# Other tiles take the dense path, one batch's first v rows are summed by TensorE in column groups, and the dense weights are built during the queries

## The reference, cut to what matters

```
z = rmsnorm(x) @ w_in          # pool channels | q | k | v | gate_pool | gate_attn
x += (sigmoid(gate_pool) * (pool(z) @ w_pool_out) + sigmoid(gate_attn) * (attention(q,k,v) @ w_attn_out)) @ w_out
h = rmsnorm(x)                 # the expert layer, per token:
q = h @ w_query                # 8 heads, two halves of 128
s = q . sub_keys               # 16 halves x 128 scores; top 16 of each half, then top 16 of the sums
idx, gate = top16, softmax     # 8 heads x 16 = 128 experts of 16384
x += sum_k gelu(h . expert_u[idx_k]) * gate_k * expert_v[idx_k]
y = rmsnorm(x)
```

## Time and profile before

| | us |
|---|---|
| median of three runs | 3104.01 (3103.43 to 3106.72) |
| the profiled execution | 3107.14 |
| its span, first to last instruction | 3105.3 |

### The profile page before, as it was taken

One profiled execution on the slowest core, in us unless ns is written; L12 is line 12 of the kernel. 1 busy time (PEld: TensorE's weight loads), 2 busy tenths in 40 slices (PEclk: granted clock), 3 DMA queues, 4 the chain that ended last, 5 costly groups with the idle time before them and its releaser, 6 DMA issues.

```text
span 3105.3 us, 34626 instructions
## 1 busy us (share of the span) xinstructions
PE 2701.4 (87%) x9441; PEld 1579.9 (51%) x9441; DVE 2230.3 (72%) x4681; ACT 572.9 (18%) x983; POOL 1633.7 (53%) x1444
## 2 busy tenths in 40 slices
PE   7989989793455867949799899999999999999997
PEld 6885566472133445524366555555555545545553
DVE  1446678999988777998888677777777766655554
ACT  2322401210034101112266211111111111100001
POOL 0001553366677776557522566666666656645441
PEclk9999999896666888969899999999999999999999
DMA  4385796788789998877677999999999999998894
GB/s 149 115 250 176 253 372 231 256 298 295 247 309 321 328 380 331 273 229 273 216 267 268 342 401 402 403 399 402 389 395 390 368 382 403 401 333 322 327 322 164
DMA packets 360702, 961.16 MB, mean 310 GB/s; under 512 B 28064, under 2 KB 152736, under 8 KB 359072
## 3 DMA queue, kind: packets, MB, share of 16 engines
q0 software_dynamic: 184320, 671.17, 58.9%
q1 hardware_dynamic: 175136, 284.69, 26.4%
q10 hardware_dynamic: 1152, 4.19, 0.3%
HBM read 930.58 MB, written 29.36 MB: 309 GB/s over the span
## 4 chain that ended last, share of the span: by engine, by line
PE 62%; DVE 21%; issue 5%; DMA 5%; ACT 4%; POOL 3%; POOLq 0%; ACTq 0%; SPq 0%; DVEq 0%
PE o_bank L778 21%; PE bank L788 21%; PE bank L550 9%; DVE ring L1116 8%; PE bank L538 5%; DMA ring<-in_expert_u,idx_now 3%; POOL ring L1083 2%; PE bank L724 2%; PE o_bank L759 2%; DVE region_q L1347 2%; DVE region_q L1352 2%; DVE region_q L1356 2%; DMA wslot<-in_expert_uT 1%; ACT region_q L983 1%; PE bank L528 1%
## 5 line engine op out<-in xcount | busy, mean ns | idle before, releaser
L1083 POOL DMA_INDIRECT ring<-in_expert_u,idx_now x640 | 783.9, 1225 | 432.8 <-DVE dots L1116 196.1
L1083 POOL DMA_INDIRECT ring<-in_expert_v,idx_now x640 | 744.3, 1163 | 472.7 <-issue 152.3
L778 PE MATMUL o_bank<-region_b,wslot 128*128 128x384 f32 x2048 | 686.5, 489 | 17.0 <-DMA wslot<-in_expert_uT 17.0
L788 PE MATMUL bank<-wslot,region_q 128*128 128x512 f32 x1536 | 679.9, 592 | 0.0
L1116 DVE CUSTOM_DVE_ANT_0 ring<-ring,h 128x1024 f32<-128x1024 f32 x512 | 608.1, 1221 | 73.6 <-DMA ring<-in_expert_u,idx_now 61.0
L1429 DVE SCALAR_TENSOR_TENSOR region_c<-ring,dots,region_c 128x1024 f32<-128x1024 f32 x384 | 493.0, 1284 | 100.4 <-DMA ring<-in_expert_v,idx_now 60.3
L778 PEld LDWEIGHTS o_bank<-region_b,wslot 128*128 128x128 f32 x2048 | 391.4, 191 | 318.9 <-issue 63.6
L788 PEld LDWEIGHTS bank<-wslot,region_q 128*128 128x128 f32 x1536 | 291.8, 190 | 340.3 <-issue 306.6
L1075 POOL COPY idx_now<-idx 128x8 uint32 x160 | 105.4, 659 | 519.6 <-DVE idx L1358 286.3
L724 PE MATMUL bank<-ring,region_s 128*128 128x512 f32 x512 | 246.0, 610 | 57.2 <-ACT region_s L961 47.0
L1003 ACT ACTIVATE region_q<-o_bank 128x384 f32<-128x384 f32 x128 | 62.9, 491 | 982.8 <-PE o_bank L778 939.7
(11 more groups left out here) (163 smaller groups left out, 2363.5 us busy)
## 6 DMA issues: line engine op xcount, KB each, us to landing
wslot<-in_expert_uT SPq DMA_DIRECT2D x128, 512.0 KB
wslot<-in_expert_v SPq DMA_DIRECT2D x128, 512.0 KB
wslot<-in_w_in SPq DMA_DIRECT2D x34, 1024.0 KB
wslot<-in_w_query SPq DMA_DIRECT2D x24, 1024.0 KB
region_p<-expert_weights SPq DMA_DIRECT2D x20, 768.0 KB
wslot<-in_w_out SPq DMA_DIRECT2D x12, 1024.0 KB
expert_weights<-region_q SPq DMA_DIRECT2D x6, 2048.0 KB, 7.4
expert_weights<-region_p SPq DMA_DIRECT2D x6, 2048.0 KB, 7.4
```

What stands on the lines that cost most here:

```text
L778: ins = nc.tensor.matmul(dense_in[q][:, 0:DENSE_T], u_cols[slot][:, k, :], h2T[:, k, T - DENSE_T:T], start=(k == 0), stop=(k == KD - 1))
L788: ins = nc.tensor.matmul(dense_out[2 * t + n][:], hidden[q][:, t * P:(t + 1) * P], v_cols[slot][:, n * 512:(n + 1) * 512], start=start, st ...
L1083: nc.gpsimd.indirect_dma_start(ring[:, r, :], None, table, bass.IndirectOffsetOnAxis(ap=idx_now[:, half, r:r + 1], axis=0)).then_inc(row_l ...
```

## The change

The tiles are divided anew. Gathered are now tiles 0 and 1 of batch 0 and tiles 0 to 2 of batch 1, dense are tiles 2 and 3 of batch 0 and tile 3 of batch 1: five and three, as before.

- The u and v rows of the two gathered tiles of batch 0 are all handled ahead of the columns. The order on POOL is u0, v0, u1, v1 and then u2, u3, u4, v2, v3, v4 beside the columns: 512 rows ahead of them and 768 beside them (`ROWS_BY`: 6.14 for each of 125 columns, none for the first three).
- The v rows of the two early tiles are gathered by token: one indirect DMA brings the 128 expert rows of one token, one to a partition. The ids are turned (transposed) for that. The weights of a token then are the stationary operand of a matmul, as one column among 32, the rest zeros; four tokens, for four groups of 32 columns of the array, make a "quad" of 8 matmuls of 512 columns (`sum_rows`). 32 quads make a tile, 64 in all. They stand between batch 1's projections (24), at the end of group 1's queries (8), in batch 1's queries (18) and beside the last weights (14).
- The dense weights of the two batch-0 tiles are built between batch 1's queries (64 jobs of four tokens), those of the third after them (32 jobs). ACT issues the stores. Blocks are of 16 tokens, units of 8 columns.
- Batch 1's tile 3 is merged first; the other three merges are made beside the columns, at columns 0, 6 and 26, with one column (and its rows) at each of eight pauses (three columns in the first merge).
- POOL takes its ids straight from `idx`, with no copy to `idx_now`, and its loop is written out. Waits on one count of used rows become one semaphore for each place of the ring.

The diff, cut to its core:

```diff
-GATHERED = (TT, 1)
-BLOCK = 32
-UNIT_COLS = 4
-UNITS_BESIDE = {(0, 1): 3, (1, 0): 3, (1, 1): 4}
-SUMMED = 1
+GATHERED = ((0, 0), (0, 1), (1, 0), (1, 1), (1, 2))
+DENSE = ((0, 2), (0, 3), (1, 3))
+EARLY = 2
+GATHERS = [("u", 0), ("v", 0), ("u", 1), ("v", 1), ("u", 2), ("u", 3), ("u", 4), ("v", 2), ("v", 3), ("v", 4)]
+BLOCK = 16
+UNIT_COLS = 8
+QUARTERS = 4
+SUM_BUFS = 4
+FIRST_ROWS = 3
+ROWS_BY = [max(0, (j - FIRST_ROWS + 1) * LATE_ROWS // (N_KEYS - FIRST_ROWS)) for j in range(N_KEYS)]
+MERGE_AT = {6: 3, 26: 4}
...
+            def sum_rows(*key):
...
+                for r in quads:
+                    rows = [ROW["v", k] + QUARTERS * r + q for q in range(QUARTERS)]
+                    for n in rows:
+                        landed(pe, n)
+                    pe.wait_ge(sum_w_ready, k * QUADS + r + 1)
+                    for half in range(2):
+                        for q, n in enumerate(rows):
+                            ins = nc.tensor.matmul(sums[half][q * QUAD_ROWS:(q + 1) * QUAD_ROWS, :],
+                                                   sum_w[:, r % SUM_BUFS, q, QUAD_ROWS - 1 - r:2 * QUAD_ROWS - 1 - r],
+                                                   ring[:, n % RING, half * 512:(half + 1) * 512],
+                                                   start=(r == 0), stop=(r == QUADS - 1), skip_group_check=True)
...
                 for c in range(HALVES // 2):
                     for hp in (2 * c, 2 * c + 1):
                         feature_major((g, "query", hp), (g, "query", c), h2T, hp % 2 * P, KD)
+                        builds(c, hp % 2)
...
+                        builds(c, 2 + hp % 2)
+                    if WT_AFTER.get(g) == c:
+                        turn_weights(g, g - 1)
+                    sum_rows("query", g, c)
...
-                                nc.gpsimd.tensor_copy(
-                                    idx_now[:, half, :],
...
+            def column():
...
+                j = columns[0]
+                weigh_column()
+                rows(ROWS_BY[j] - (ROWS_BY[j - 1] if j else 0))
...
-            attn_out(1, 3)
+            pool_out(1, 1)
             attention(1, 1)
+            attn_out(1, 6)
             out(1, 3)
...
-            merge(0, 3, 6)
-            rotate(1, 3)
-            pool_out(2, 3)
-            attention(2, 3)
-            attn_out(2, 7)
-            out(2, 5)
+            merge(0, 3)
+            rotate(1)
+            pool_out(2, 2)
+            add_sums(0)
+            split_ids(0)
+            attention(2, 1)
+            attn_out(2, 6)
+            out(2, 4)
             norm2(2)
...
+            merge(1, 3)
+            softmax(1, slice(3, 4))
+            split_ids(2)
+            for n in range(2 * JOBS_PER_TILE, W_JOBS):
+                one_hots(n)
+            add_sums(1)
+            norm2_again(4)
+            pauses = iter(range(8))
+            merge(1, 0, lambda: column() if next(pauses) in (3, 5, 7) else None)
+            while columns[0] < N_KEYS:
+                if columns[0] in MERGE_AT:
+                    merge(*GATHERED[MERGE_AT[columns[0]]], column)
+                else:
+                    column()
```

More of the change, by code:

```diff
@@ new lines @@
+LATE_SUMS_AT = {**{("query", 2, c): 3 for c in range(2, 8)}, ("h2D",): 4, ("chosen",): 2, **{("w", n): 1 for n in range(67, 96, 4)}}
+SUMS_BEFORE, SUMS_OF = {}, {}
+for _k, _table in enumerate((SUMS_AT, LATE_SUMS_AT)):
+    _n = 0
+    for _key, _count in _table.items():
+        SUMS_BEFORE[_key], SUMS_OF[_key] = (_k, _n), (_k, range(_n, _n + _count))
+        _n += _count
+    assert _n == QUADS and max(_table.values()) <= SUM_BUFS
+FIRST_ROWS = 3
+LATE_ROWS = (len(GATHERED) - EARLY) * 2 * SLOTS
@@ L554, in turn_h, with build_weights @@
+            def build_weights(n):
+                g = LAST_GROUP[1]
+                pe.wait_ge(one_hot_ready, n + 1)
+                bank = fill(g, "w", n)
+                for r in range(TOKENS_EACH):
+                    at1 = n % 2 * TOKENS_EACH + r
+                    ins = nc.tensor.matmul(bank[:, r * P:(r + 1) * P], one_hot_i[:, at1, :], one_hot_j[:, at1, :],
+                                           start=True, stop=True)
+                done(ins, g, "w", n)
             def turn_h(g):
@@ L769, in take_column @@
+            sum_rows("h2D")
+            turn_chosen(2)
+            sum_rows("chosen")
+            for n in range(2 * JOBS_PER_TILE, W_JOBS):
+                build_weights(n)
+                sum_rows("w", n)
             def take_column(j, slot, turn):
@@ new lines, in dot, with add @@
+                dotted[0] += count
+            added = [EARLY * SLOTS]
+            def add(count):
+                for d in range(added[0], added[0] + count):
+                    k, s = divmod(d, SLOTS)
+                    b, t = GATHERED[k]
+                    n = ROW["v", k] + s
+                    landed(dve, n)
+                    if s:
+                        used(dve, n - 1)
+                    x = x1s[b][:, t, :]
+                    nc.vector.scalar_tensor_tensor(out=x, in0=ring[:, n % RING, :],
+                                                   scalar=dots[:, DOTS_AT[k] + s:DOTS_AT[k] + s + 1], in1=x,
+                                                   op0=ALU.mult, op1=ALU.add).then_inc(slot_used[n % RING], 1)
+                added[0] += count
@@ L1132, in norm1, with rows @@
+            def rows(count):
+                dots_left = min(count, len(GATHERED) * SLOTS - dotted[0])
+                dot(dots_left)
+                add(count - dots_left)
             def norm1(b):
@@ new lines, in weigh, with add_sums @@
+            def weigh(k):
+                b, t = GATHERED[k]
+                dve.wait_ge(gelu_ready, k + 1)
+                d = dots[:, DOTS_AT[k]:DOTS_AT[k] + SLOTS]
+                nc.vector.tensor_tensor(d, d, gate[:, b, t, :], ALU.mult).then_inc(weighed, 1)
+                dve.wait_ge(weighed, k + 1)
+            def add_sums(k):
+                b, t = GATHERED[k]
+                all_used(dve, ("v", k))
+                for half in range(2):
+                    x = x1s[b][:, t, half * 512:(half + 1) * 512]
+                    n = step(nc.vector.tensor_tensor(x, x, sums[half], ALU.add))
+                after(n)
+                dve.sem_inc(sums_added, 1)
@@ L1528, in _ @@
-            dot(4)
-            norm2(2)
-            dot(8)
-            for hp in range(HALVES):
-                top_halves(2, hp)
-                dot(4)
-            dot_to(GATHERED[0] * SLOTS // BODY)
-            softmax(0)
-            weigh(0)
-            for t in range(TT):
-                merge(1, t)
-            softmax(1)
-            for t in range(GATHERED[1], TT):
-                split_ids(t)
-            for block in range(BLOCKS):
-                one_hots(block)
-            add_sums()
```

824 lines of the change are left out of this document (442 added, 382 removed).

## The result

The changed kernel takes 3016.72 us (median of four runs, 3012.2 to 3028.44), the kernel before 3105.36 beside it: a ratio of 0.9721, interval 0.9692 to 0.9749. It is faster by 89 us, where 200 were forecast. The range ended at 3010. Its profiled execution takes 3016.6 us with a span of 3014.8.

What follows compares the result with a forecast made beforehand. PE bounded the columns before, waits the front; after, DMA at 400 to 412 GB/s would pace the columns. Fourth column's add at 1492, plus 1388, 5 and a tail of 20 gave 2905 us; range 2805 to 3010.

Steps and rivals of the forecast that it cites:

- attention of batch 1 starts: Front, after group 1, batch 1's projections, rotate and pool_out: attention was to start at 854 us instead of 868.9.
- the queries: Batch 1's queries with weight jobs and quads: 230 us instead of 125.1, from 1101 to 1331.
- from there to the fourth column's add: Last halves, merge, third tile's 32 weight jobs and first columns: from 1331 to column 3's add at about 1492.
- the columns from there: 125 columns, paced by DMA: 1388 us, 109 at 10.95 and 16 at 12.1, plus 5 for the last add.
- the price that decides most: PE time of one quad of 8 matmuls: 1.7 us if its four column groups run together; 64 quads cost 110 us.
- the ends of 3.4 and 6.9: Quad price in us if column groups run only in pairs (3.4, chance 0.06) or one after another (6.9, chance 0.05).
- 6 x 30: Six query chunks of batch 1 with three quads each, taken at 30 us; with 2 x 24.8 the queries' 230.
- sixth rival: Ahead of the columns: DVE, PE and ACT tied more closely than summed, a late row stopping PE; +60 us, 2965, chance 0.13.
- Group 1: Its attn_out +17 us from added dots; its queries about 116 us instead of 94.9, with 8 quads.
- rival 3: Columns: u loads behind doubled units, or rows in the ring of eight, come late; 11.8 us a column, +93, 2998, chance 0.14.
- if PE waits for `wslot` every eight columns: Columns: one of the signs in the profile after that would show the prediction wrong; no size given.
- The merges' price: Merges at columns 6 and 26: 35 us of DVE each beside 8 columns, 97 us, 12.1 a column.

Runs made afterwards that it cites:

- spread kernel: Changed kernel with batch 1's late quads spread singly, one behind three of four steps of query chunks 1 to 7: 2971.48 us, ratio 0.9563 to the kernel before.
- the kernel whose bytes don't bind: Changed kernel gathering only half of each of the 768 rows beside the columns, dots taken with h2 alone, instruction counts unchanged: 2910.77 us, one run.
- the quarters alone: Changed kernel with each large unit load of dense weights split into four DMAs, issued with four successive columns: 2996.19 us, ratio 0.9684 to the kernel before.

## Why the prediction was wrong

The forecast span was 2905, the measured one 3014.8. By its own steps:

| | forecast | measured | difference |
|---|---|---|---|
| attention of batch 1 starts | 854 | 877.6 | +24 |
| attention, `attn_out`, `out` to the queries | 247 | 238.8 | -8 |
| the queries | 230 | 289.1 | +59 |
| from there to the fourth column's add | 161 | 176.5 | +15 |
| the columns from there | 1393 | 1419 | +26 |
| the tail | 20 | 14 | -6 |

**The quad**, called the price that decides most, was right: 1.7 us forecast, 1.92 measured, far from the ends of 3.4 and 6.9. An estimate by the ratio of the Trainium skill, page TensorE: Matmul & The Clock Gate (Measured speedup vs the span model), was 2.2; four groups here run 6.9 / 1.92 = 3.6 times as fast as one after another, nearer to the 4x of its page TensorEngine Tiling (Array Packing) (Theoretical Speedup).

**The queries are the step that failed.** The prediction priced a chunk by PE's instructions ("6 x 30") and checked the rows only as a rate in front ("a quad needs 4 x 1.45 = 5.8 us of POOL and comes every 8.6 us or so"). In the queries quads do not come every 8.6 us: three come at once, then none for 25 us, and the ring of eight rows can hold two of them ready. The third costs a fresh round of issue and landing, a wait of 8.7 us, and 1.7 more at half the clock: chunks of 41 to 43 us instead of 30, five times. The spread kernel shows that the sum itself was sound: with the quads apart a chunk is 30.2 us and the queries 233, as forecast. A late row was in my sixth rival ("a row late stops PE", +60) only as a mixture of several ties, and the size of the ring only in the third, for the columns; in the queries it was one tie, in one place.

**Behind the queries** it is the same term. The six quads ahead of the third tile's weights were given nothing. They wait for their rows, the ids are turned only behind the first four of them (at 1458, although the merge has written them by 1443), and two more stand between the ids and the jobs (to 1471.8). The eight beside the weights were priced at PE's time; there the jobs took 67 us, close to the 61 forecast.

**The front.** Group 1 was 18 us late at its end: behind `attn_out` PE goes on at 435.8, 25 us later than before, where 17 were forecast, and its queries took 124 us for 116. The projections took 199.5 us instead of 185: 21 quads at PE's pace of 9.0 us with their jobs. Behind them DVE's part took 49 instead of 58. The shape was right, the sizes a few per cent short. Two small sums in the prediction are off by 2 us each: its terms give 852 for the start of attention, not 854, and 1099 for the start of the queries, not 1101.

**The columns** came out near the forecast in length, but by another path, so the nearness is in part luck. The bytes were right and the rate too high: 4.47 MB a column at 390 GB/s is 11.46 us; the takes give 1419 / 125 = 11.35, against 11.1 in my sum (1388 / 125). The measured rates of 380 to 393 over all columns at full bytes stand below my 400 to 412. The Trainium skill's DMA: Bandwidth & Descriptors (Where 436 GB/s comes from) has about 358 for HBM and one core, which the trace exceeds over the columns. The path was rival 3's and not the forecast's: the u load late behind a unit, as described, with 0.14 and a price of 93 us. PE waited 94.5 us in 12 such waits, and this sign ("if PE waits for `wslot` every eight columns") had been named as one of being wrong, while PE waited only 12 us for DVE's weighed columns. But doing away with it gives back less, since PE then waits for rows by way of DVE: the quarters alone took 11 us off (intervals overlapping), beside the spread quads 32. The merges' price was right: 99.6 and 94.2 us for the eight columns that hold one, in the kernel whose bytes don't bind, against 97.

**The range** ended at 3010, just short. Its high end gave each rival little beside another, and two came true together: the delays ahead of the columns came to 90 us, beyond the 60 of rival 6, and the mechanism of rival 3 was there too, with 26 us over my sum instead of 93.

## What to carry to other kernels

When work that eats from a ring is put beside other work, price it twice: by the engine's instructions, and by the round of the ring for what comes in one burst (places / need), since the mean rate says nothing of a burst larger than the ring. Spread such consumers so that no burst needs more than the ring holds; here the same instructions in another order, with the weight loads cut into quarters, took 93 us off, and putting five of them under a wait that was there anyway 13 more. Before moving work out of a wait, look at who ends the stage: a wait that lies under another engine's chain is the best place for it.

## What the runs showed of the hardware

A stall of PE costs more than its length. In the changed kernel 11 of the 12 waits for a u load are of 2.3 to 12.5 us. Behind each of them PE's first matmuls run at a granted clock of 0.50, the lower of its two levels (1.2 GHz), and the column takes 11.9 to 13.3 us instead of 10.31. Behind the twelfth, of 0.9 us, the clock is at 1.00 and the column takes 10.4. Busy time of ten microseconds with the wait, and of the ten behind it:

```profile
2030.00:2040.00 10.00, 4.58 (x11) 1.71 (x9) 8.38 (x15) 0.00 (x0) 7.98 (x7) 0.90 1.04 392
2040.00:2050.00 10.00, 4.16 (x7) 2.35 (x8) 2.47 (x4) 0.00 (x0) 5.14 (x5) 0.50 1.03 406
```

A DMA issue on SP can itself take long. The u load's issue took 7.10 us behind a unit load of 0.79 MB and 23.45 us behind one of 1.57 MB, and at most 7.4 us behind a quarter of it. The size of the load ahead is not all: behind the same 1.57 MB, but with half of the rows' bytes beside it, the issue took 6.3 to 9.2 us in 14 places.
